# A hybrid encoder layer on one core: whole 128-token chunks in the recurrence, and rotation partners by transfer

## The reference, cut to what matters

```python
z = x @ w_in                        # q,k,v,r of the recurrence, ga, attention q,k,v, memory q, gates
log_a = log_sigmoid(ga @ w_gla_a2 + b_gla_a) / 16
# recurrence, 4 heads of 128x128, S_t = diag(a_t) S_{t-1} + k_t^T v_t, o_t = q_t S_t, in blocks:
b = cumsum(log_a)                   # within a block
q_dec, k_inv, k_tail = q * exp(b), k * exp(-b), k * exp(b_last - b)
o = tril(q_dec @ k_inv^T) @ v + q_dec @ S
S = S * exp(b_last) + k_tail^T @ v
o_a = rms_norm(o) * silu(r)
# sliding-window attention, 8 query and 2 key-value heads of 64; first 16 of 64 dims are rotated:
rot = concat(x1 * cos - x2 * sin, x2 * cos + x1 * sin)      # x1, x2 of 8 dims each
# cross-attention into 256 memory tokens; merge by gates, w_o, LN, gated conv FFN, LN
```

## Time and profile before

| | us |
|---|---|
| median of 3 runs | 1824.6 (1824.24 to 1826.39) |
| the profiled execution's own time | 1824.12 |
| its span | 1822.3 |
| PE busy / PEld busy | 1797.4 / 1720.4 |
| DVE / ACT / POOL busy | 978.6 / 706.9 / 233.4 |
| mean granted clock of TensorE | 0.997 |

### The profile page before, as it was taken

How to read it: one execution, slowest core, us unless ns; L and a number is a source line. 1 busy time by engine, 2 the same in 40 slices (tenths; PEclk the granted TensorE clock), 3 DMA queues, 4 the chain that set the end, 5 groups by cost and what they waited for, 6 DMA issues and landing times.

```text
span 1822.3 us, 31470 instructions
## 1 busy us (share of the span) xinstructions
PE 1797.4 (99%) x12084; PEld 1720.4 (94%) x12084; DVE 978.6 (54%) x1362; ACT 706.9 (39%) x1259; POOL 233.4 (13%) x334
## 2 busy tenths in 40 slices
PE   8999999999999999999999999999999999999997
PEld 7999999999999889989998889999999999999997
DVE  3111143443323376656657579777777776654564
ACT  3122333323312355556333135544454444443342
POOL 0000000000011110000000003333332332001011
PEclk9999999999999999999999999999999999999999
DMA  5111111212231231122445323222222221884762
GB/s 164 46 46 46 39 60 56 76 55 73 64 107 47 81 100 48 47 60 89 141 142 198 93 64 94 91 73 82 70 70 88 75 82 65 254 280 153 227 218 82
DMA packets 181290, 179.63 MB, mean 99 GB/s; under 512 B 20828, under 2 KB 149149, under 8 KB 181212
## 3 DMA queue, kind: packets, MB, share of 16 engines
q1 hardware_dynamic: 179356, 172.56, 31.1%
q0 software_dynamic: 1856, 5.99, 0.9%
HBM read 143.08 MB, written 35.53 MB: 98 GB/s over the span
## 4 chain that ended last, share of the span: by engine, by line
PE 94%; DVE 3%; ACT 1%; issue 1%; DMA 0%; POOL 0%; SPq 0%; ACTq 0%; POOLq 0%; DVEq 0%
PE banks L1469 23%; PE banks L1011 18%; PE banks L1012 18%; PE banks L1013 18%; PE banks L1426 5%; PE banks L1263 1%; PE banks L1280 1%; PE banks L1243 1%; PE banks L1275 1%; PE banks L1248 1%; PE banks L1129 1%; PE banks L1133 1%; PE banks L1097 1%; PE banks L1182 0%; PE banks L1149 0%
## 5 line engine op out<-in xcount | busy, mean ns | idle before, releaser
L1011 PE MATMUL banks<-act_hi,w_hi 128*128 128x352 f32 (+1 forms) x1200 | 400.3, 334 | 1.4 <-DVE act_lo L2129 1.3
L1012 PE MATMUL banks<-act_lo,w_hi 128*128 128x352 f32 (+1 forms) x1200 | 389.5, 325 | 0.0
L1013 PE MATMUL banks<-act_hi,w_lo 128*128 128x352 f32 (+1 forms) x1200 | 389.5, 325 | 0.0
L2115 DVE TENSOR_TENSOR w_lo<-w_raw,w_hi 128x1024 fp32r<-128x1024 f32 x70 | 85.9, 1227 | 353.1 <-ACT w_hi L1572 353.1
L1011 PEld LDWEIGHTS banks<-act_hi,w_hi 128*128 128x128 f32 x1200 | 226.3, 189 | 14.9 <-issue 9.3
L1469 PE MATMUL banks<-x_free_r,a_hi 128*128 128x256 f32 x1232 | 226.8, 282 | 0.8 <-DVE a_lo L2442 0.5
L1012 PEld LDWEIGHTS banks<-act_lo,w_hi 128*128 128x128 f32 x1200 | 226.4, 189 | 1.2
L1013 PEld LDWEIGHTS banks<-act_hi,w_lo 128*128 128x128 f32 x1200 | 226.4, 189 | 0.0
L1469 PEld LDWEIGHTS banks<-x_free_r,a_hi 128*128 128x128 f32 x1232 | 190.1, 188 | 1.3 <-DVE x_free_r L2468 0.7
L1469 PE MATMUL banks<-xs_hi,a_hi 128*128 128x274 f32 x616 | 178.8, 290 | 1.6 <-DVE xs_lo L2468 1.0
L1469 PE MATMUL banks<-xs_lo,a_hi 128*128 128x274 f32 x616 | 178.4, 290 | 0.0
(11 more groups left out here) (311 smaller groups left out, 3378.9 us busy)
## 6 DMA issues: line engine op xcount, KB each, us to landing
w_raw<-in_w_down SPq DMA_DIRECT2D x112, 256.0 KB, 3.5
w_raw<-in_w_in SPq DMA_DIRECT2D x100, 256.0 KB, 3.3
gate_in<-gates_scratch SPq DMA_DIRECT2D x24, 529.0 KB, 3.7
h_keep<-conv SPq DMA_DIRECT2D x22, 530.0 KB, 2.7
w_raw<-in_w_up SPq DMA_DIRECT2D x44, 256.0 KB, 4.0
x_free<-in_w_up SPq DMA_DIRECT2D x44, 256.0 KB, 3.7
h_raw<-h_keep SPq DMA_DIRECT2D x22, 384.0 KB, 5.1
gates_scratch<-gate_st SPq DMA_DIRECT2D x32, 176.0 KB, 1.9
```

The source lines that it names most:

```text
L1011: pe.matmul(out, hi, b_hi, start=start, stop=False)
L1012: pe.matmul(out, hi, b_lo, start=False, stop=False)
L1013: return pe.matmul(out, lo, b_hi, start=False, stop=stop)
L2115: dve.tensor_tensor(dst[:, :, :], w_raw[slot][:, :, :], src[:, :, :].bitcast(F32), ALU.subtract).then_inc(q.w_split_lo, 1)
```

## The change

The recurrence works in blocks of 128 tokens, so each full tile is one block: one state product over 128 tokens, one state share of 128 columns, one update of the state in place. The scores are made from factors taken about the middle of the block (`q_mid`, `k_mid`), which are two more differences and exponentials. The sums of squares (L1154) stand between fill 4 and fill 5. The sample's initial state is loaded at the very start by POOL into `S_b`, not after tile 7. The middle exponentials and `e_t` stand ahead of fill 1 on ACT; on DVE `split(0)` stands ahead of `er + 1`, `split(1)` at the end of the tile.

The rotation's matmuls, their matrix and its load are gone. SP copies the partner rows (four transfers of 8 rows x 1058 columns a chunk, on-chip) into a cleared buffer `rot`, sin carries the sign, and DVE and POOL work on whole chunks. The core of the diff:

```diff
...
-    causal = (s <= t) & (s // BLK == t // BLK)
+    causal = s <= t
...
-            sin[base + h:base + h + half] = np.sin(ang)
+            sin[base + h:base + h + half] = np.sin(ang) if h else -np.sin(ang)
...
-    rope_t = [m.take(f"rope_t{i}", [P, GW], F32) for i in range(2)]
+    rot = [m.take(f"rot{i}", [P, TT], F32) for i in range(2)]
...
+        def rope_rows(k):
+            c = ROPE_CHUNKS[k]
+            sp.wait_ge(q.proj_free, rope_ready(c))
+            if k >= 2:
+                sp.wait_ge(q.rope_done, k - 1)
+            for base in (0, SWA_HD):
+                for to, of in ((base, base + 8), (base + 8, base)):
+                    sp.dma_start(rot[k % 2][to:to + 8, :], z[of:of + 8, c, :]).then_inc(rot_landed[k % 2], 16)
+        sp.wait_ge(q.rot_cleared, 1)
+        rope_rows(0)
+        rope_rows(1)
         for i in range(4):
             cols(T_MQ // 2 + i, 0, w_in, C_MQ + i * P)
             mem_tile(T_MQ // 2 + i, 1, 0, i)
+            if i == 0:
+                rope_rows(2)
+                rope_rows(3)
+            if i == 1:
+                rope_rows(4)
...
+        pool.dma_start(S_b[:, :, :], I["state_gla"][0, 0].rearrange("h k v -> k h v")).then_inc(q.state_in, 16)
...
-        pool.dma_start(S_b[:, :, :], I["state_gla"][0, 0].rearrange("h k v -> k h v")).then_inc(q.state_in, 16)
...
-        pool.wait_ge(q.att_consts, 48)
-        for k in range(15):
-            c = ROPE_CHUNKS[k // 3]
-            g0, w = GROUPS[k % 3]
-            pool.wait_ge(q.rope_mm, k + 1)
-            pool.tensor_tensor(z[:, c, g0:g0 + w], z[:, c, g0:g0 + w], cos[:, g0:g0 + w], ALU.mult).then_inc(q.rope_cos, 1)
...
+        pool.wait_ge(q.att_consts, 32)
+        for k in range(5):
+            c = ROPE_CHUNKS[k]
+            pool.wait_ge(rot_landed[k % 2], rot_count(k))
+            pool.tensor_tensor(z[:, c, :], z[:, c, :], cos[:, :], ALU.mult).then_inc(q.rope_cos, 1)
...
-            pe.wait_ge(q.qdec_ready, t + 1)
-            pe.wait_ge(q.kinv_ready, t + 1)
+            pe.wait_ge(q.factors_done, t * 4 + 2)
+            pe.wait_ge(q.factors_done, t * 4 + 3)
             pe.wait_ge(q.att_ready, t)
             for h in range(H):
-                pe.matmul(bank4(5)[0:w, h, 0:w], k_inv[:, h, 0:w], q_dec[:, h, 0:w], start=True, stop=True)
-            pe.wait_ge(q.ktail_ready, t + 1)
+                pe.matmul(bank4(5)[0:w, h, 0:w], k_mid[:, h, 0:w], q_mid[:, h, 0:w], start=True, stop=True)
+            pe.wait_ge(q.factors_done, t * 4 + 4)
             pe.wait_ge(q.vtok_ready, t + 1)
             for h in range(H):
                 last = pe.transpose(bank4(4)[0:w, h, :], k_tail[:, h, 0:w], ident[:, :])
             last.then_inc(q.kt_turned, 1)
             fill(3)
+            pe.wait_ge(q.kttok_ready, t + 1)
+            pe.wait_ge(q.state_end, t)
+            for h in range(H):
+                last = pe.matmul(bank4(7)[:, h, :], kt_tok[0:w, h, :], v_tok[0:w, h, :], start=True, stop=True)
+            last.then_inc(q.ds_mm, 1)
             pe.wait_ge(q.att_ready, t + 1)
             pe.wait_ge(q.o_normed, t)
-            pe.wait_ge(q.state_end, t)
+            for h in range(H):
+                pe.matmul(bank4(6)[:, h, 0:w], v_tok[0:w, h, :], att[0:w, h, 0:w], start=(h == 0), stop=False,
+                          skip_group_check=True)
+            pe.wait_ge(q.factors_done, t * 4 + 1)
             if w < P:
                 pe.wait_ge(q.state_in, 16)
-            pe.wait_ge(q.kttok_ready, t + 1)
-            c, n = blocks[0]
             for h in range(H):
-                last = pe.matmul(bank4(7)[:, h, :], kt_tok[c:c + n, h, :], v_tok[c:c + n, h, :], start=True, stop=True)
-            last.then_inc(q.dsa_mm, 1)
-            for h in range(H):
-                pe.matmul(bank4(6)[:, h, 0:w], v_tok[0:w, h, :], att[0:w, h, 0:w], start=(h == 0), stop=False,
-                          skip_group_check=True)
-            for h in range(H):
-                last = pe.matmul(bank4(6)[:, h, c:c + n], s_in[:, h, :], q_dec[:, h, c:c + n], start=False,
-                                 stop=len(blocks) == 1, skip_group_check=True)
-            if len(blocks) == 1:
-                last.then_inc(q.o_mm, 1)
+                last = pe.matmul(bank4(6)[:, h, 0:w], state[:, h, :], q_dec[:, h, 0:w], start=False, stop=True,
+                                 skip_group_check=True)
+            last.then_inc(q.o_mm, 1)
             fill(4)
-            if len(blocks) == 2:
-                c, n = blocks[1]
-                pe.wait_ge(q.state_mid, t + 1)
-                for h in range(H):
-                    last = pe.matmul(bank4(6)[:, h, c:c + n], s_out[:, h, :], q_dec[:, h, c:c + n], start=False,
-                                     stop=True, skip_group_check=True)
-                last.then_inc(q.o_mm, 1)
-                for h in range(H):
-                    last = pe.matmul(bank4(7)[:, h, :], kt_tok[c:c + n, h, :], v_tok[c:c + n, h, :], start=True, stop=True)
-                last.then_inc(q.dsb_mm, 1)
-            fill(5)
             pe.wait_ge(q.osq_ready, t + 1)
             pe.matmul(bank4(3)[:, :, 0:w], ones[:, :], osq4[:, :, 0:w], start=True, stop=True).then_inc(q.rms_mm, 1)
+            fill(5)
...
-        def rope_turn(k):
-            c, (g0, w) = ROPE_CHUNKS[k // 3], GROUPS[k % 3]
-            pe.wait_ge(q.proj_free, rope_ready(c))
-            if k >= 2:
-                pe.wait_ge(q.rope_sin, k - 1)
-            pe.matmul(bank(2 + k % 2)[:, 0:w], turn[:, :], z[:, c, g0:g0 + w], start=True, stop=True).then_inc(q.rope_mm, 1)
...
-            act.activation(e_p[:, :, 0:w], bank4(3)[:, :, 0:w], ACT.Exp).then_inc(q.epos_ready, 1)
-            act.activation(e_n[:, :, 0:w], bank4(3)[:, :, 0:w], ACT.Exp, scale=-1.0).then_inc(q.eneg_ready, 1)
+            act.activation(e_p[:, :, 0:w], bank4(3)[:, :, 0:w], ACT.Exp).then_inc(q.exps_done, 1)
+            act.wait_ge(q.diffs_done, t * 2 + 1)
+            act.activation(k_mid[:, :, 0:w], q_mid[:, :, 0:w], ACT.Exp).then_inc(q.exps_done, 1)
+            act.wait_ge(q.exps_done, t * 4 + 2)
+            act.activation(q_mid[:, :, 0:w], q_mid[:, :, 0:w], ACT.Exp, scale=-1.0).then_inc(q.exps_done, 1)
+            act.wait_ge(q.diffs_done, t * 2 + 2)
+            act.activation(e_t[:, :, 0:w], e_t[:, :, 0:w], ACT.Exp).then_inc(q.exps_done, 1)
             act.wait_ge(q.state_end, t)
-            act.activation(decay[:, :, 0:blocks], bank4(3)[:, :, bl - 1:w:bl], ACT.Exp).then_inc(q.decay_ready, 1)
+            act.activation(decay[:, :, :], bank4(3)[:, :, w - 1:w], ACT.Exp).then_inc(q.decay_ready, 1)
             fill(1)
-            act.wait_ge(q.diff_ready, t + 1)
-            act.activation(e_t[:, :, 0:w], e_t[:, :, 0:w], ACT.Exp).then_inc(q.etail_ready, 1)
+            act.wait_ge(q.v_turned, t + 1)
+            act.wait_ge(q.o_mm, t)
+            act.activation(v_tok[0:w, :, :], bank4(4)[0:w, :, :], ACT.Copy).then_inc(q.vtok_ready, 1)
...
-            act.wait_ge(q.v_turned, t + 1)
-            act.wait_ge(q.dsb_mm, t)
-            act.activation(v_tok[0:w, :, :], bank4(4)[0:w, :, :], ACT.Copy).then_inc(q.vtok_ready, 1)
             fill(2)
             fill(3)
-            fill(4)
             act.wait_ge(q.o_mm, t + 1)
             act.activation(osq4[:, :, 0:w], bank4(6)[:, :, 0:w], ACT.Square).then_inc(q.osq_ready, 1)
-            fill(5)
+            fill(4)
             act.wait_ge(q.rms_mm, t + 1)
             act.activation(lnms4[:, :, 0:w], bank4(3)[:, :, 0:w], ACT.Ln, bias=eps[:, 0:1]).then_inc(q.lnms_done, 1)
             act.wait_ge(q.lnms_done, t + 1)
             act.activation(rstd4[:, :, 0:w], lnms4[:, :, 0:w], ACT.Exp, scale=-0.5).then_inc(q.rstd_ready, 1)
...
-            if blocks == 2:
...
-            dve.tensor_tensor(dd, bb[:, :, bl - 1:bl].to_broadcast([P, H * blocks, bl]), bb, ALU.subtract).then_inc(q.diff_ready, 1)
-            dve.wait_ge(q.epos_ready, t + 1)
             dve.wait_ge(q.o_mm, t)
+            bb = b_s[:, :, 0:w]
+            dve.tensor_tensor(q_mid[:, :, 0:w], bb[:, :, mid:mid + 1].to_broadcast([P, H, w]), bb, ALU.subtract).then_inc(q.diffs_done, 1)
+            dve.tensor_tensor(e_t[:, :, 0:w], bb[:, :, w - 1:w].to_broadcast([P, H, w]), bb, ALU.subtract).then_inc(q.diffs_done, 1)
+            dve.wait_ge(q.exps_done, t * 4 + 1)
             dve.scalar_tensor_tensor(q_dec[:, :, 0:w], z[:, 0:4, bass.ds(c, w)], GLA_SCALE, e_p[:, :, 0:w], ALU.mult, ALU.mult)\
-                .then_inc(q.qdec_ready, 1)
-            dve.wait_ge(q.eneg_ready, t + 1)
-            dve.tensor_tensor(k_inv[:, :, 0:w], z[:, 4:8, bass.ds(c, w)], e_n[:, :, 0:w], ALU.mult).then_inc(q.kinv_ready, 1)
-            dve.wait_ge(q.etail_ready, t + 1)
-            dve.tensor_tensor(k_tail[:, :, 0:w], z[:, 4:8, bass.ds(c, w)], e_t[:, :, 0:w], ALU.mult).then_inc(q.ktail_ready, 1)
+                .then_inc(q.factors_done, 1)
+            dve.wait_ge(q.exps_done, t * 4 + 2)
```

(79 more changed lines are left out.)

43 lines of the change are left out of this document (17 added, 26 removed).

## The result

The changed kernel takes **1795.35 us** (median of 4 runs, 1795.16 to 1797.74), the kernel before 1825.07 in the same comparison (1824.24 to 1826.39): ratio 0.9839, 95% interval 0.9822 to 0.9857. The profiled execution took 1795.27 us with a span of 1793.5.

The account below looks back on a forecast made before the run. PE, busy 1797.4 of 1822.3 us, was taken as the bound. Recurrence 18.8 plus rotation 9.0 less 0.8 at the start gave 27.0 us off 1824.12, 1797.1; with 0.5 for the runs' median, 1797.6, range 1796 to 1804.

Parts of the forecast that it names:

- Step 1: Recurrence, 8 full tiles: the second half-block's state share and state product leave PE, 2.01 us and 0.03 more a tile.
- Step 2: Recurrence: the first half-block's three PE groups get 128 rows and columns, 2.86 us for 3.15, 0.29 less a tile.
- Step 3: Recurrence: the norm's sums of squares (L1154) move ahead of fill 5; no cost, as fill 4 hides the wait.
- Step 4: Recurrence: PE's wait for DVE's `la` ahead of L1097 goes, 0.05 us a tile.
- Step 5: Recurrence: the tile's new ACT and DVE work stays hidden from PE, the masked scores by 1.6 us.
- Step 6: Rotation before the attention scores: its 15 matmuls go, on-chip transfers and DVE and POOL passes replace them; 9.0 us saved.
- Step 7: Kernel start: the state's early load goes in front of tile 3 of x in full DMA queues; 0.8 us lost.
- rows don't matter: Recurrence: the 64-row groups' excess belongs to their place in the stream and stays; 1801.1 us, chance 0.13.
- Given back: Attention units: PE arrives early and waits for ACT and DVE, returning the rotation's 9.0 us; 1806.6 us, chance 0.04.
- A new wait: Recurrence tile: masked scores or `la` late by 1 us beyond their slack, 8 times; 1805.6 us, chance 0.07.
- The start costs more: Kernel start: longer idle time brings a second low-clock stretch, 1.7 us more; 1799.3 us, chance 0.10.
- the slower one: Rotation: partner rows land late, DVE's low split follows late and PE stands; 1829.6 us at 6.4 late each, chance 0.04.

Follow-up runs that it names:

- run 6: Changed kernel with the norm's row sums (L1154) back behind fill 5 on PE and ACT: 1800.96 us, tile 31.16.
- run 3: Changed kernel whose state product uses only the first 64 tokens of a block (64 rows of weights): 1797.93 us, tile 31.19.
- Run 5: Changed kernel whose state share is added only to the first 64 tokens of a block (64 moving columns): 1797.87 us, tile 30.81.
- run 4: Changed kernel with ACT's Ln and Exp of the norm behind fill 5 again, PE's stream unchanged: 1807.14 us, tile 32.03.
- run 7: Changed kernel with DVE's reciprocal ahead of the turned keys and masked scores instead of behind them: 1824.18 us.
- run 10: Changed kernel with every 8-row transfer of the rotation's partner rows cut into eight of one row, 160 issues instead of 20: 1832.52 us.

## Why the prediction missed its range: the recurrence's term was too small

The term that failed is the recurrence's: 18.8 us forecast, 20.95 measured. With the measured one the forecast would have been 1795.45. The mechanism was as forecast, and three of the sizes in it were not: steps 1, 2 and 4. A middle tile got 2.66 us shorter where 2.35 was reckoned. The first two tiles gave only 2.50 and 2.54: the first one's wait for `la` stayed, and the second had had almost none.
- **Step 1**, 2.04 a tile. From fill 4's end to the next gate it was 0.93 + 1.08 + 4.01 + 0.95 us and is 0.46 + 4.38: 2.13 less. I had held that changes between dense and small groups stay six, and they do. But an interruption of the dense stream costs about 0.10 beyond its groups (fills 4 and 5 take 7.97 with a group between them and 7.87 run through in run 6), and the norm's new one is paid for by its parting from the 33-row gate. Missed: 0.09.
- **Step 2**, 0.29 a tile, with 0.10 charged for the doubled columns. It came to 0.37 to 0.39. The gain from full height is confirmed (run 3 gives 0.38 back), though not as the prediction put it: the 64-row records themselves are as fast as others, and the excess lies in the changes of the number of rows. Run 5 shows that moving columns cost nothing. I took the 0.82 and 0.92 of two groups for the price of columns, when the 0.92 was lengthened by a wait. Missed: 0.09.
- **Step 3**, nothing: right (run 6).
- **Step 4**, 0.05 a tile. The wait cost 0.05 ahead of the group and 0.11 in it, 0.16 in all (the rows of before and after, runs 4 and 6). It is the same 0.92 misread: I used it as the clean length of a group. Missed: 0.11.
- **Step 5**, hidden: right. The masked scores end at 327.95 and are wanted at 329.60, 1.65 us where 1.6 was reckoned; run 7 confirms the cover of 1.4 for the keys.
- **Step 6**, 9.0: 9.02. The rows' landing, for which there was no measurement, was taken as 2 to 3 us; POOL's passes, which wait for it, began 1.8 to 3.1 us after a chunk's last issue, and the first chunk was done with 4.6 us to spare. The issues were dearer, 0.67 us apart against 0.47.
- **Step 7**, 0.8: x landed 0.92 later, and the recurrence began 0.63 later, which owes something to where the low-clock stretch fell. The forecast lies between them.

Rivals: "rows don't matter" is out (run 3). "Given back" is out: the part behind the scores is 0.5 us longer, and the 14 profiles lie within 1 us there. "A new wait" didn't come. "The start costs more" was seen in four profiles with the early load, not in the profiled pair. Of the slower one, DVE's waiting for rows is real, and beside it stands the late weight load; they begin somewhere between 2.7 and 19 us of SP's queue a chunk (run 10), and where was not tried.

The range's lower end, 1796, came from 19.0 for the recurrence and 9.0 for the rotation with nothing lost at the start, 1796.6. So it allowed 0.2 us for an error of the main term in that direction, while its upper end allowed 3.5 (15.3 for that term). A like distance below would have held the result.

## What to carry to other kernels

Where PE is 99% busy, value a group from its neighbours' starts, and take as the clean length only one whose operands were early: a group behind a wait is longer inside too. In this kernel float32 groups with weights of 128 columns ran at one pace, 0.112 us a record, whether 32, 64 or 128 columns moved and whether 32, 64 or 128 rows were loaded. So blocks of half the size saved nothing on PE, and each change of the number of weight rows cost 0.19 us; padding a 33-row matmul with zeros was faster than leaving it small. A wait of 2 us on a busy TensorE must be priced with the clock that it may bring down.
